# Experts ordered by their token counts, and the state-space prelude laid out anew, in a decoder step on one core

## The reference

```python
def s5_ssm(u, h0, a_re, a_im, log_dt, b_re, b_im, c_re, c_im, d_skip):
    lam = lax.complex(a_re, a_im)
    dt = jnp.exp(log_dt)[:, None]
    a_bar = jnp.exp(lam * dt)
    b_bar = ((a_bar - 1.0) / lam)[..., None] * lax.complex(b_re, b_im)
    bu = jnp.einsum('gnc,bsgc->bsgn', b_bar, u)
    ...   # states by h[t] = a_bar * h[t-1] + bu[t]
    y = jnp.einsum('gcn,bsgn->bsgc', c, states).real + d_skip * u

def moe(h, w_router, b_router, w1, b1, w2, b2):
    logits = h @ w_router + b_router
    top_v, top_i = lax.top_k(logits, 4)
    gates = jax.nn.softmax(top_v)
    ...   # for each expert e and each of its tokens
    a = h @ w1[e] + b1[e]
    mid = min(a_glu, 7) * sigmoid(1.702 * min(a_glu, 7)) * (clip(a_lin, -7, 7) + 1)
    out += gate * (mid @ w2[e] + b2[e])
```

## Time and profile before

| | us |
|---|---|
| median of 3 runs (lowest, highest) | 1381.19 (1380.71, 1382.87) |
| the profiled execution | 1380.01 |
| its span, first to last instruction | 1378.2 |
| busy in it: TensorE, VectorE, ScalarE, GpSimd | 1168.2, 570.8, 225.1, 96.7 |

### The profile page before, as it was taken

How to read it: one execution, slowest core, us unless ns; L and a number is a source line. 1 busy time by engine, 2 the same in 40 slices (tenths; PEclk the granted TensorE clock), 3 DMA queues, 4 the chain that set the end, 5 groups by cost and what they waited for, 6 DMA issues and landing times.

```text
span 1378.2 us, 25532 instructions
## 1 busy us (share of the span) xinstructions
PE 1168.2 (85%) x8826; PEld 455.9 (33%) x8827; DVE 570.8 (41%) x1280; ACT 225.1 (16%) x434; POOL 96.7 (7%) x198
## 2 busy tenths in 40 slices
PE   5898788989987889998899899889999677689884
PEld 4665444443321323332233223323332222133221
DVE  4899744344332433333333333344333222244333
ACT  3002443021110111111111111111111100011112
POOL 1667400000000000000000000000000000000000
PEclk9999999969998999999999999999999988999997
DMA  8324593750899999989978997997839999968993
GB/s 262 110 77 141 165 352 132 268 215 14 355 422 423 423 422 423 397 333 423 398 309 338 423 392 315 423 423 300 365 158 423 422 422 422 423 288 364 395 421 133
DMA packets 77901, 444.94 MB, mean 323 GB/s; under 512 B 16560, under 2 KB 17392, under 8 KB 26640
## 3 DMA queue, kind: packets, MB, share of 16 engines
q1 hardware_dynamic: 77872, 444.58, 79.9%
HBM read 442.04 MB, written 2.51 MB: 323 GB/s over the span
## 4 chain that ended last, share of the span: by engine, by line
PE 58%; DMA 12%; DVE 9%; SPq 8%; issue 7%; DVEq 2%; ACT 2%; POOL 1%; ACTq 0%
PE ps L1444 20%; PE ps L1430 9%; SPq L421 8%; PE ps L1453 7%; DMA mixer<-in_w_moe_dram 6%; PE ps L1460 5%; DMA ring<-in_w_moe_dram 4%; PE ps L1472 3%; PE ps L1350 2%; PE ps L1116 2%; DMA uni<-in_w_moe_dram 2%; PE ps L1468 1%; PE ps L1485 1%; DVE uni L1063 1%; PE ps L1412 1%
## 5 line engine op out<-in xcount | busy, mean ns | idle before, releaser
L1444 PE MATMUL ps<-ring,uni 128*32 128x512 f32 x2496 | 287.5, 597 | 14.0 <-DMA ring<-in_w_moe_dram 14.0
L1033 DVE TENSOR_TENSOR x<-x,ps 128x1024 f32<-128x1024 f32 x158 | 186.8, 1209 | 13.8 <-PE ps L1430 7.2
L1430 PE MATMUL ps<-uni 64*128 64x512 f32 x624 | 174.3, 665 | 4.2 <-issue 2.9
L1054 DVE TENSOR_SCALAR uni<-ps 128x256 f32<-128x256 f32 x51 | 21.7, 425 | 342.9 <-PE ps L1444 342.9
L1460 PE MATMUL ps<-uni 128*32 128x256 f32 x1224 | 91.4, 440 | 79.2 <-issue 79.2
L1444 PEld LDWEIGHTS ps<-ring,uni 128*32 128x32 f32 x2496 | 79.3, 110 | 205.6 <-issue 172.1
L697 ACT ACTIVATE uni<-uni 128x256 f32<-128x256 f32 x51 | 21.2, 416 | 528.0 <-DVE uni L1054 528.0
L1453 PE MATMUL ps<-ring,uni 128*32 128x512 f32 x768 | 89.6, 597 | 20.4 <-DVE uni L1063 16.6
L1430 PEld LDWEIGHTS ps<-uni 64*128 64x128 f32 x624 | 55.4, 200 | 104.3 <-issue 101.5
L1460 PEld LDWEIGHTS ps<-uni 128*32 128x32 f32 x1224 | 40.6, 122 | 145.7 <-issue 132.5
L697 ACT ACT_TABLE_LOAD x51 | 65.4, 1283 | 79.7 <-issue 79.3
(11 more groups left out here) (338 smaller groups left out, 1188.8 us busy)
## 6 DMA issues: line engine op xcount, KB each, us to landing
ring<-in_w_moe_dram SPq DMA_DIRECT2D x258, 1024.0 KB, 20.6
tmp<-in_w_moe_dram SPq DMA_DIRECT2D x42, 1024.0 KB, 24.8
w_glu<-in_w_moe_dram SPq DMA_DIRECT2D x21, 1024.0 KB, 26.2
mixer<-in_w_moe_dram SPq DMA_DIRECT2D x21, 1024.0 KB, 25.4
accT<-in_w_moe_dram SPq DMA_DIRECT2D x21, 1024.0 KB, 23.0
uni<-in_w_moe_dram SPq DMA_DIRECT2D x21, 1024.0 KB, 24.6
ring<-in_w_in_dram SPq DMA_DIRECT2D x4, 2048.0 KB, 13.0
ring<-in_cache_k_dram SPq DMA_DIRECT2D x8, 1024.0 KB, 5.1
```

Source lines behind the costliest of these rows:

```text
L1033: tt(rows(t), rows(t), ps[0:TILES[t][1], b0:b0 + 2, :], ALU.add).then_inc(S["acc"], 1)
L1430: ins = mm(ps[:, b0 + c, :], selT[rows, P * t:P * t + P], y[rows, :], start=True, stop=True)
L1444: ins = mm(hidden(q), xe[:, k % 2, quarter(k // 2)], columns(slot(turn, k), q), start=False, stop=(k == 7), skip_group_check=True)
```

## The change

Three parts of the program are altered.

*Order of the experts.* Two constant rows and columns give ties and places. After the totals VectorE ranks the experts by tokens (ties by number; experts 0 and 1 fixed in front), compares ranks with the list `places()`, and a matmul of the resulting 0-1 table spreads the experts' names and counts, in the new order, to `names_o` and `cnt`. Ranks stand so that heavy experts lie far apart (by the reversed bits of the place). SP loads the names of the next two experts into registers for its refills, VectorE that of the current one for its tables of positions and gates.

*The parameter chain.* Transposes of the A parameters come after four features, not after all; their reduction, exponential and sines come ahead of the last features' evictions. C and old states follow all features.

*B and the angles.* The B transposes come after three blocks of projection, not four, and ScalarE evicts them. GpSimd stops after level 3 of the angle table; levels 4 to 6 are VectorE's alone, both halves.

```diff
+    e = np.arange(NEXP)
+    tie = np.where(e < FIXED, 1e5 - e, NEXP - 1 - e)
+    c[:, C_TIE:C_TIE + NEXP] = tie
+    c[0:NEXP, C_COL], c[0:NEXP, C_COL + 1] = tie, e
+    c[:, C_PLACE:C_PLACE + NEXP] = places()
     return c
+def places():
+    spread = sorted(range(NEXP - FIXED), key=lambda i: int(format(i + 1, "05b")[::-1], 2))
+    rank = list(range(NEXP))
+    for r, i in enumerate(spread):
+        rank[FIXED + i] = FIXED + r
+    return np.array(rank)
...
+        def expert_at(eng, place):
+            return eng.value_load(names_o[0:1, bass.ds(place, 1)], min_val=0, max_val=NEXP - 1)
+        def run_experts(eng, block_of, named=False):
             done = eng.alloc_register()
             eng.reg_mov(done, 0)
             def expert(turn, e, before):
                 count = eng.value_load(cnt[0:1, bass.ds(e, 1)], min_val=1, max_val=NTOK)
+                name = expert_at(eng, e) if named else None
                 with eng.Fori(0, 3) as o:
                     with eng.If(count > o * (3 * CAP)):
                         with eng.Fori(0, 3) as c:
                             with eng.If(count > o * (3 * CAP) + c * CAP):
                                 n = eng.snap(done, min_val=0, max_val=NEXP * CHUNKS)
-                                block_of(n, turn, e, before, o * (3 * CAP) + c * CAP)
+                                block_of(n, turn, name, before, o * (3 * CAP) + c * CAP)
...
-            def refill(turn, e, k, ahead):
+            def refill(turn, following, k, ahead):
                 if k < NPIECE - 1:
                     sp.wait_ge(S["w_used"], ahead * (NPIECE - 1) + (k + 1))
                 else:
                     sp.wait_ge(S["w_last"], ahead + 1)
                 later, k2 = divmod(k + NSLOT, NPIECE)
-                sp.dma_start(slot(turn, k), piece(e + later, k2)).then_inc(landed(turn, k), 16)
+                sp.dma_start(slot(turn, k), piece(following[later - 1], k2)).then_inc(landed(turn, k), 16)
...
+                    following = [expert_at(sp, e + 1), expert_at(sp, e + 2)]
                     for k in range(NPIECE):
-                        refill(turn, e, k, ahead)
+                        refill(turn, following, k, ahead)
...
-            for level in range(7):
+            for level in range(4):
                 m = 1 << level
                 re, im = e_tab[:, 0, :, 0:m], e_tab[:, 1, :, 0:m]
                 cr = bc(e_tab[:, 0, :, m - 1:m], [P, NI, m])
                 ci = bc(e_tab[:, 1, :, m - 1:m], [P, NI, m])
                 t1, t2 = e_tmp[:, 0, :, 0:m], e_tmp[:, 1, :, 0:m]
-                if level >= 5:
-                    pool.wait_ge(S["etab_d"], level - 4)
                 link(tt(t1, re, cr, ALU.mult))
                 link(tt(t2, im, ci, ALU.mult))
-                ins = tt(e_tab[:, 0, :, m:2 * m], t1, t2, ALU.subtract)
-                if level >= 4:
-                    ins.then_inc(S["etab_p"], 1)
-                    pool.wait_ge(S["etab_p"], level - 2)
-                    continue
-                link(ins)
+                link(tt(e_tab[:, 0, :, m:2 * m], t1, t2, ALU.subtract))
...
             act.wait_ge(S["prm"], 16 * NPRM)
             A(ld[0:NI, 0:2], ld[0:NI, 0:2], ACT.Exp).then_inc(S["dt"], 1)
+            act.wait_ge(S["gmx"], 16)
+            features_out(1)
+            features_out(3)
             act.wait_ge(S["red"], 1)
             A(prm[:, PA_R, :], prm[:, PA_RD, :], ACT.Exp)
+            act.wait_ge(S["red"], 2)
             A(prm[:, PA_C, :], prm[:, 11, :], ACT.Sin)
             A(prm[:, PA_S, :], prm[:, 12, :], ACT.Sin).then_inc(S["exps"], 1)
+            features_out(5)
+            features_out(7)
             for n, c in enumerate([12, 13, 14, 15] + list(range(12))):
+                if n == 3:
+                    act.wait_ge(S["bT_ps"], 1)
+                    A(bT[:, :, :], ps[:, 0:2, :], ACT.Copy).then_inc(S["bT"], 1)
...
+            features_out(0)
+            features_out(2)
             dve.wait_ge(S["prmT"], 1)
-            link(dve.tensor_copy(prm[:, 0:4, :], ps[:, 0, 0:64].rearrange("p (a i) -> p a i", a=4)))
+            dve.tensor_copy(prm[:, 0:4, :], ps[:, 0, 0:64].rearrange("p (a i) -> p a i", a=4)).then_inc(S["red"], 1)
+            dve.wait_ge(S["red"], 1)
...
+            features_out(4)
+            features_out(6)
+            dve.wait_ge(S["prmT"], 2)
...
             def angle_level(level):
                 m = 1 << level
-                dve.wait_ge(S["etab_p"], level - 3)
                 re, im = e_tab[:, 0, :, 0:m], e_tab[:, 1, :, 0:m]
+                cr, ci = (bc(e_tab[:, r, :, m - 1:m], [P, NI, m]) for r in range(2))
                 t1, t2 = (e_tmp_v[:, a].rearrange("p (i t) -> p i t", i=NI)[:, :, 0:m] for a in range(2))
-                tt(t1, re, bc(e_tab[:, 1, :, m - 1:m], [P, NI, m]), ALU.mult)
-                link(tt(t2, im, bc(e_tab[:, 0, :, m - 1:m], [P, NI, m]), ALU.mult))
-                return tt(e_tab[:, 1, :, m:2 * m], t1, t2, ALU.add)
+                t3, t4 = (e_tmp[:, a, :, 0:m] for a in range(2))
+                tt(t1, re, cr, ALU.mult)
+                tt(t2, im, ci, ALU.mult)
+                tt(t3, re, ci, ALU.mult)
+                link(tt(t4, im, cr, ALU.mult))
+                tt(e_tab[:, 0, :, m:2 * m], t1, t2, ALU.subtract)
+                return tt(e_tab[:, 1, :, m:2 * m], t3, t4, ALU.add)
             dve.wait_ge(S["fdone"], 1)
-            for level in (4, 5):
-                angle_level(level).then_inc(S["etab_d"], 1)
-                dve.wait_ge(S["etab_d"], level - 3)
-            dve.wait_ge(S["bT_ps"], 1)
-            dve.tensor_copy(bT[:, 0, :], ps[:, 0, :])
-            dve.tensor_copy(bT[:, 1, :], ps[:, 1, :]).then_inc(S["bT"], 1)
+            dve.wait_ge(S["etab_p"], 1)
+            link(angle_level(4))
+            link(angle_level(5))
             angle_level(6).then_inc(S["etab_v"], 1)
...
-            ts(cnt[:, :], ps[:, 1, 96:128], 1.0, None, ALU.max).then_inc(S["cntr"], 1)
-            link(ts(nblk[:, 0, :], ps[:, 1, 96:128], 1.0, (CAP - 1) / 2, ALU.max, ALU.add))
+            stt(put[:, 0, :], ps[0:NEXP, 1, 96:128], float(NEXP), tie_row, ALU.mult, ALU.add)
+            link(stt(rank[:, 0:1], ps[0:NEXP, 1, 128:129], float(NEXP), tie_col, ALU.mult, ALU.add))
+            link(ts(put[:, 1, :], put[:, 0, :], rank[:, 0:1], None, ALU.is_gt))
+            link(dve.tensor_reduce(rank[:, 1:2], put[:, 1, :], AX, ALU.add))
+            link(ts(put[:, 1, :], place_row, rank[:, 1:2], None, ALU.is_equal))
+            ts(put[:, 2, :], put[:, 1, :], name_col, None, ALU.mult)
+            ts(put[:, 3, :], put[:, 1, :], ps[0:NEXP, 1, 128:129], None, ALU.mult).then_inc(S["gates"], 1)
+            dve.wait_ge(S["gT_ps"], 2)
+            dve.tensor_copy(names_o[:, :], ps[:, 1, 192:224])
+            ts(cnt[:, :], ps[:, 1, 224:256], 1.0, None, ALU.max).then_inc(S["cntr"], 1)
...
+            for j in range(4):
+                features(j)
...
+            pe.wait_ge(S["rows"], 1)
+            for a, src in enumerate((par[0:NI, 0:P], par[0:NI, P:2 * P], st_out[0:NI, 0, :], st_out[0:NI, 1, :])):
+                ins = tp(ps[:, 0, NI * a:NI * a + NI], src, ident[0:NI, 0:NI])
+            ins.then_inc(S["prmT"], 1)
+            for j in range(4, J):
+                features(j)
...
-            for n in range(4):
+            for n in range(3):
                 project(n)
             pe.wait_ge(S["crev"], 1)
             pe.wait_ge(S["fdone"], 1)
...
                 for b in range(4):
                     ins = tp(ps[:, r, P * b:P * b + P], xb[:, r, P * b:P * b + P], ident)
             ins.then_inc(S["bT_ps"], 1)
+            project(3)
             pe.wait_ge(S["bT"], 1)
...
+            for u in range(3):
+                m = TILES[u][1]
+                ins = mm(ps[0:NEXP, 1, 128:129], rt_s[0:m, u, 1, :], ones[0:m, 0:1], start=(u == 0), stop=(u == 2))
             ins.then_inc(S["posps"], 1)
             pe.wait_ge(S["gates"], 1)
             for t, (t0, n) in enumerate(TILES):
                 ins = tp(ps[0:NEXP, 4, t0:t0 + n], rt_s[0:n, t, 2, :], ident[0:n, 0:n])
             ins.then_inc(S["gT_ps"], 1)
+            pe.wait_ge(S["gates"], 2)
+            mm(ps[:, 1, 192:256], ones[0:NEXP, :], put[:, 2:4, :], start=True, stop=True).then_inc(S["gT_ps"], 1)
```

More of the change, by code:

```diff
@@ L570, in _, with features_out @@
             A(st[:, 3:6], st[:, 3:6], ACT.Sqrt).then_inc(S["rt"], 1)
[L572 to L573 removed]
+            def features_out(j):
                 act.wait_ge(S["xT_ps"], j + 1)
@@ L1087, in _, with features @@
             pe.wait_ge(S["xn"], 1)
-            for j in range(J):
+            def features(j):
                 if j >= 4:
```

41 lines of the change are left out of this document (19 added, 22 removed).

## The result

The changed kernel takes **1345.0 us** (median of 4 runs, 1344.1 to 1345.4) against 1381.5 (4 runs, 1380.7 to 1382.9) for the kernel before in the same comparison: ratio 0.9734, 95% interval 0.9717 to 0.9751. The forecast was 1342, the range 1333 to 1354. Its profiled execution is one of 1345.3 us with a span of 1343.5; before it was 1380.0 with 1378.2.

The account below looks back on a forecast made before the run. It took the expert stage, three quarters of the kernel, as bounded by TensorE and by DMA's late pieces behind a full ring. 1380.0 - 7.7 (prelude) + 2.3 (routing) - 32.5 (order) = 1342.1; forecast 1342, range 1333 to 1354.

Parts of the forecast that it names:

- The order term: Expert stage: spreading heavy experts apart removes waits for weight pieces, 32.5 us less, bounds 30 and 36.
- the rule for the clock: Expert stage: TensorE's clock falls to half behind a wait, making the next pass 1.3 us longer.
- My variant: Expert stage: clock also falls behind two light experts in five; old order 1052.8 us, new 1021.9, 31 less.
- The recurrence: Expert stage: pass-by-pass count of piece waits through the 18-piece ring; 1048.4 us in old order, 1014.7 in new.
- The name's load: VectorE's register load at each expert switch: 0.6 us, hidden under 0.83 us of idleness, so 0 cost.
- Routing: Router, ahead of the second biases: extra small matmuls and VectorE ranking cost 2.3 us, bounds 1.7 and 3.5.
- The prelude: State-space part before VectorE's loop of 16 groups: loop moves 7.7 us earlier, bounds 5.5 and 10.6.
- The cap: Prelude: VectorE, ready 10.6 us earlier, gains only TensorE's 5.5 plus 2.15 slack, 7.7 us.
- The name's load is on the path: Rival, expert switches: 31 loads of 0.6 us cost 19 us, giving 1361; 7 in 100.
- slower: Rival, expert switches: loads of 2.2 us on the path cost 68 us, giving 1410; 2 in 100.
- the order brings nothing: Rival, expert stage: DMA at its limit whatever the order, only the front moves, 1375; 4 in 100.
- More than forecast: Rival: 36 from order, 10.6 from prelude, 1.7 for routing give 1335 to 1336; under 1333, 9 in 100.

Follow-up runs that it names:

- Experiment 3: Changed kernel with the experts from 2 on in plain order of their counts, heaviest first: 1443.8 us.
- 1: Changed kernel with the experts run in the order of their numbers, all else kept: 1371.4 us.
- experiment 10: Changed kernel with only half the columns of each refilled weight piece transferred: 1307.5 us.
- experiment 5: Changed kernel with one loop per expert, in steps of 32 to its count, instead of two nested loops, on every engine: 1337.4 us.
- experiment 11: Changed kernel with one loop per expert and half of each refilled weight piece left out: 1211.8 us.
- 2: Changed kernel with only the new prelude kept: experts in number order, no ranking, names or extra register loads: 1373.4 us.
- experiment 4: Changed kernel with one or two more, unused loads of the expert's name on VectorE at each switch: 1344.8 and 1342.4 us.
- experiment 8: Changed kernel with levels 4 to 6 of the angle table shared between GpSimd and VectorE again: 1348.4 us.
- 9: Changed kernel with the B transposes evicted by VectorE again, in two copies between angle levels 5 and 6: 1346.1 us.

## Why the prediction was right, and where it was not

**The bound of the expert stage** was read rightly: pieces that come late because DMA stood still behind a full ring. Experiment 3 moved the time by 100 us with the order alone, 1 gave back what the change had gained, 10 took the waits away with the bytes.

**The order term was too large: -26.3 instead of -32.5**, outside its bounds of 30 to 36. I sort the excess of the passes into those in which a piece was waited for and the rest:

| | old order | new order | difference |
|---|---|---|---|
| waiting passes, forecast | 81 | 47.5 | -33.5 |
| waiting passes, trace | 72.1 | 40.3 | -31.8 |
| other passes, forecast | 1.5 | 1.5 | 0 |
| other passes, trace | 7.2 | 12.8 | +5.6 |

The waiting passes are too dear by 7 to 9 us in both orders, so that their difference came out nearly right. **The step that failed is the rule for the clock**: "A pass that had to wait is followed by one that is 1.3 us longer". The dips don't need a wait ahead of them. In the changed kernel TensorE loses 1.4 to 2.6 us at places 2, 9, 11, 13, 19 and 23, none of them behind a waiting pass; with half pieces, where next to nothing is waited for, the sum is 18.4 instead of 19.1 us (experiment 10). What goes ahead of them is TensorE's idle 2.4 to 3.3 us at a switch, and with one loop, which has no such idle time, 2.3 us are left, at four times the waits (experiment 5). The clock falls there too, but inside passes that DMA paces; without late pieces it is 1.00 from 305 us to the end of the stage (experiment 11). Such an idle stretch doesn't always bring the clock down: behind 3.24 us ahead of place 15 and 3.17 ahead of place 21 of the changed kernel it stays at 1.00 and nothing is lost. What tells the two cases apart stays open. The old order suffers less from the dips, as I read it, because it has as many light experts, but more of them in passes that wait anyway, where a lost microsecond is one less to wait. The new order puts them where TensorE is the bound. The +5.6 is of one pair of traces, and this part varies: sorted in the same way, the other passes hold some 4 to 12 us in the three traces of the old order (before, experiments 1 and 2) and 9 to 19 in five of the new one (changed, 4, 8 and 9). My variant, in which the clock falls behind light experts too, had this mechanism: it gave 1021.9 for the new order (trace: 1021.8) but 1052.8 for the old one (1048.1), and I took nearly the middle of the two.

The recurrence's 1048.4 against 1048.1 on the old order was no proof of its parts: too much in the waiting passes, too little in the others and in the base (966 for 969). I could have sorted the passes of the trace before in the same way.

**The name's load** was sized at 0.6 us and is 0.61, hidden as forecast. But the 0.83 us that I took as its slack is VectorE's wait for the end of the gather. What the load may use up before TensorE's gather starts later is the time from the selection's end to that start, at the same switch 768.36 - 766.76 = 1.60 us. With the load the slack is thin in places: at the switch shown in experiment 4 the selection ends 0.9 us ahead of the gather, of which one more load leaves 0.3.

**Routing**: +1.8 for +2.3, in its bounds.

**The prelude: -9.5 for -7.7**, inside its bounds of 5.5 to 10.6. VectorE's chain was costed nearly right, 45.44 for 44.3; of the missing 1.1 us some 0.7 are three coefficient operations, 0.64 to 0.67 us each instead of the usual 0.42 while GpSimd still works on its levels. The cap that I put on it, TensorE's bu at 42.4 and group 3's product as what the scan waits for, didn't bite: bu started at 41.04, since four projections at full clock take 16.1 us and not 17.3, and then the 64 small sample matmuls took 2.04 instead of 3.17. TensorE's next bu so starts at 51.91 instead of 59.92, 8.0 earlier; with the slack of 2.15 that allows 10.2, more than VectorE's 9.4. So the gain is VectorE's own. The clock at 46 to 54 was full, as forecast.

Errors of opposite sign (+6.2 for the order; -1.8, -0.5 and -0.6 for prelude, routing and tail) left the sum 3 us off. That it came so close is luck; with the order's error alone the forecast would have been 6 off, still inside the range.

**The rivals.** "The name's load is on the path" and "slower" fall with experiments 1, 2 and 4; "the order brings nothing" with 1 and 3. "More than forecast" needed the 36 of the upper bound.

## What to carry to other kernels

With a ring of prefetched pieces and units of unequal work, sum per unit what DMA and what the computing engine take, and walk the ring's stock through the order: the time moves by what DMA stands still, and an engine's saved microseconds come back as waits where the stock is empty (92 saved, 85 given back in experiment 5). When a model meets the total, check it against the trace term by term before using it on another order. Before sharing vector work with GpSimd, compare twice the operations on VectorE alone: here six at 1.2 us beat three at 2.5 to 3.3.

## What the runs showed of the hardware that I had not expected

A switch between experts in run-time loops costs TensorE 1.0 to 3.2 us of idleness in two nested loops of three turns (up to 4.9 where the last piece came late), and next to nothing in one loop to a register's value (75.3 against 1.7 us over the kernel). Behind many of the longer ones the granted clock falls to its lower level, 1.2 GHz, and the next pass loses 1.3 to 2.7 us more.
VectorE's 128x1024 operations on SBUF take 1.22 us alone and 2.53 to 3.25 beside GpSimd's, whose own then take 1.89 to 3.21.
The Trainium skill, SBUF — State Buffer, Terms, calls the pair of ports that these two engines share an exclusive lock, under which the loser blocks for the whole instruction; the trace of experiment 8 agrees: GpSimd's three long operations end at 41.21, 44.05 and 47.34, and VectorE's beside them at 42.30, 45.13 and 48.41, each 1.07 to 1.09 us later, about the 1.22 that it takes alone.
